# Ten dot products of the adaptive parameters of a two-block model, moved from the first block into the second

## The chip, the cores and the metric

The kernel runs on one core of a Trainium2 chip: TensorE (PE) for matmuls, VectorE (DVE), ScalarE (ACT) and GpSimd (POOL) for the rest, SyncE (SP) for most of the loads. The metric is the device time of one execution in microseconds.

## The reference, cut to what matters

Two transformer blocks follow each other on 256 tokens of width 2048. The second block scales and shifts its inputs by parameters that depend on a condition vector alone, not on the tokens: `silu(cond) @ w + b`, for the condition `c` of the latent tokens and `c_ctx` of the context tokens, for each of two layers.

```python
def ada_params(cond, w, b):                      # w: 2048 x 6144, for each of two layers
    mod = jax.nn.silu(cond) @ w + b
    return jnp.split(mod, 3, axis=-1)            # shift, scale, gate

x = first_block(x, ...)       # projections, rotary attention, a recurrence, output product,
                              # then expert rows chosen by a search and gathered from two tables
for layer in range(2):        # second block
    sh_l, sc_l, g_l = ada_params(c, ada_w[layer], ada_b[layer])
    sh_c, sc_c, g_c = ada_params(c_ctx, ada_w[layer], ada_b[layer])
    xm_l = x_lat * (1.0 + sc_l) + sh_l           # scale and shift: needed before the projections
    xm_c = x_ctx * (1.0 + sc_c) + sh_c           # context: layer 0 only
    ...                                          # l_q, l_k, l_g, l_v, l_u, l_o, l_zp, l_z, mixing
    x_lat = layer_norm(ALPHA * x_lat + g_l * (y_l @ w_out), ...)   # gate: needed only at the end
```

The parameters of one layer are 6144 numbers, 48 groups of 128: groups 0 to 15 are the shift, 16 to 31 the scale, 32 to 47 the gate. The context has no use for its gate.

## The kernel before

The adaptive weights lie in memory transposed, as tiles of 128 parameters by 2048. Tile (layer, k) holds group k of a layer, 1 MB. A tile's product with a condition vector is one instruction on DVE, `tensor_tensor_reduce` in `ada_dots` (L2074 to L2090), which the profile shows at L2088 as `CUSTOM_DVE_ANT_0` with a short `DVE_READ_ACCUMULATOR2_ANT` behind it. A tile whose third entry in `ADA_SEQ` is True is *dual*: it is multiplied by both condition vectors, in two instructions. Any other tile has one. There are 96 tiles, 32 of them dual, so 128 instructions whatever the order.

`ADA_SEQ` is the order of the tiles, `ADA_FIRST` says how many are worked off at each of twelve places of the first block's DVE code, and `ADA_AT` how many stand behind each of the four slots of a weight chunk in the second block. The tiles of the first block are loaded by POOL's queue (`ada_loads`, L730 to L743) into places that are free at the time, listed in `ADA_PLACE`; their number is `ADA_LAT`. From there on the tiles go through the ring: four slots of 1 MB that SP fills in one fixed order (L696 to L716) with all weights. Load n waits until what load n - 4 brought is used up; for a tile that is its dot.

The stages that matter here, in order:

- Rotary stages. DVE scales and rotates queries and keys, half of the tokens at a time (places `rope0` before, `rope1` between and `rope2` behind the halves), then copies the transposed parts head by head (L2279 to L2283). The attention's scores follow (L2298).
- Output product. Four chunks of 512 columns; PE L1021, then transposes L1098 of the new rows. DVE adds each chunk to X (`out_add`, L2332), with the dots of `w_out0` to `w_out3` between (L2339 and L2352). A matmul in full fp32 is two records in the trace.
- Query heads and search. PE L1130 and L1141; DVE takes the dots of `search` (L2366) and then chooses the top 16. The rows of two tables are gathered from there on, until about 1720 us.
- Second block. A weight is split for accuracy: ACT copies its high half (L1476), DVE subtracts to get the low half (`split_lo`, L2102; for l_u to l_z POOL does it), and PE takes three products (L903). A chunk is four slots of two pieces each. `split_lo` does for each slot: two low halves, a `conv_unit` of an earlier chunk where there is one (L2465 to L2467), then the dots of `ADA_AT`. `l_q`, `l_k` and `l_v` have two chunks each, `w_even` four. `l_g` is a small gate weight, with its dots at L2620. The weights of `l_k` and `l_v` are shared with the context's and carry the names `in_c_k` and `in_c_v` in the trace. After `w_even` the norm of `post` (L2821 to L2850) ends the layer, and the transposes L1380 begin the next.

The lines that say how the work is spread:

```python
107 ADA_SEQ = [(0, _k, True) for _k in range(16)] + [(0, _k, False) for _k in range(32, 40)]
108 ADA_SEQ += [(0, _k, True) for _k in range(16, 32)] + [(0, _k, False) for _k in range(40, 48)]
112 ADA_FIRST = {"in": 8, "in_x0": 4, "in_x1": 2, "conv": 2, "rope0": 1, "rope1": 3, "rope2": 4,
113              "w_out0": 4, "w_out1": 4, "w_out2": 4, "w_out3": 4, "search": 2}
```

## Time and profile before

| | us |
|---|---|
| median of 3 runs | 2619.73 (2617.78 to 2621.02) |
| profiled execution | 2618.13 |
| its span | 2616.3 |

| stage, from - to (us) | what runs |
|---|---|
| 0 - 150 | input projections, 16 dual tiles |
| 150 - 225 | rotary stages, eight single tiles |
| 225 - 271 | attention |
| 271 - 373 | output product, 16 dual tiles |
| 373 - 400 | first query head, search, two single tiles |
| 400 - 1720 | row gathers and their products |
| 1740 - 1860 | l_q, l_k, l_g, l_v 0 |
| 2142 - 2230 | w_even and its norm |
| 2230 - 2616 | odd layer and output |

A row of the timeline shows the start, the length, engine, line, operation and tiles, then the count, and in brackets the engine's idle time before it with what ended that. Neighbouring records on PE and DVE overlap by up to a tenth of a microsecond, so the spacing of the starts, not the length, is what one costs. A row of the chain is start, length and what it was.

### The profile page before, as it was taken

Reading aid. Unit: us, or ns where it says so; the run is one execution under the profiler, and the core shown is the slowest. Engines: PE = TensorE matmul, PEld = TensorE weight load, DVE = VectorE, ACT = ScalarE, POOL = GpSimd, SP = SyncE. Lnnn points to the kernel's source line nnn. Section 1 sums busy time; section 2 is a strip of 40 time slices with the busy share of each in tenths; the row PEclk is TensorE's granted clock in tenths of the full one; section 3 lists DMA queues with packets and bytes.
Section 4 is the critical chain, followed back from the end, with each engine's and each line's share of the span. In section 5 each row is a group of like instructions: output and inputs, shape, how many; then the busy total and the mean of one; then the engine's idle time right before and its main releaser. Section 6 shows DMA issues by size and latency. Waiting matters only on the chain.

```text
span 2616.3 us, 23133 instructions
## 1 busy us (share of the span) xinstructions
PE 2164.5 (83%) x8406; PEld 1472.8 (56%) x8406; DVE 2060.7 (79%) x2582; ACT 679.9 (26%) x1149; POOL 1131.0 (43%) x641
## 2 busy tenths in 40 slices
PE   8999999896004666778787888799999999999997
PEld 5877558655001222344443333379778887788886
DVE  6886797988997997687886777789865689777666
ACT  2054110100000000332540000133524444544343
POOL 0000003555586678767887776730255640000000
PEclk9999999898557888888779989899999999999999
DMA  9663879999999999999999999978843458777552
GB/s 377 263 263 129 331 290 375 387 421 422 407 422 421 397 408 420 420 417 407 359 310 404 393 387 370 386 290 310 321 188 129 172 204 349 292 293 289 192 202 104
DMA packets 126977, 845.16 MB, mean 323 GB/s; under 512 B 22507, under 2 KB 23019, under 8 KB 25195
## 3 DMA queue, kind: packets, MB, share of 16 engines
q0 software_dynamic: 79776, 513.13, 49.1%
q1 hardware_dynamic: 43344, 308.04, 30.9%
q10 hardware_dynamic: 3744, 22.52, 2.2%
q8 instruction: 67, 1.10, 0.2%
q14 instruction: 46, 0.38, 0.0%
HBM read 909.36 MB, written 2.10 MB: 348 GB/s over the span
## 4 chain that ended last, share of the span: by engine, by line
PE 46%; DMA 18%; DVE 16%; POOL 12%; issue 7%; ACT 1%; DVEq 0%; POOLq 0%; ACTq 0%; SPq 0%
PE psum L903 23%; DMA W<-in_peer_v,HT 7%; PE psum L1021 4%; DMA W<-in_peer_u,W 4%; POOL W L785 4%; POOL W L783 4%; DVE W L2450 3%; PE psum L859 3%; PE psum L1186 3%; PE psum L835 3%; POOL early_rows L783 3%; DMA early_rows<-in_peer_v,HT 3%; DVE early_rows L2450 2%; DMA early_rows<-in_peer_u,W 2%; DVE X L2592 2%
## 5 line engine op out<-in xcount | busy, mean ns | idle before, releaser
L1186 PE MATMUL psum<-W,HT 128*128 128x512 f32 x536 | 299.2, 711 | 311.0 <-ACT HT L1683 175.5
L903 PE MATMUL psum<-split,hi 128*128 128x512 f32 x1664 | 514.7, 390 | 3.1 <-DVE split L2102 3.1
L2450 DVE CUSTOM_DVE_ANT_0 W<-W,XN 128x2048 f32<-128x2048 f32 x148 | 335.1, 2290 | 73.3 <-DMA W<-in_peer_u,W 70.9
L1476 ACT ACTIVATE split<-ring 128x1024 fp32r<-128x1024 f32 x272 | 282.6, 1057 | 409.1 <-PE psum L903 290.3
L1186 PEld LDWEIGHTS psum<-W,HT 128*128 128x128 f32 x536 | 117.5, 228 | 479.9 <-issue 471.8
L785 POOL DMA_INDIRECT W<-in_peer_v,HT x173 | 317.3, 1834 | 91.4 <-issue 49.0
L903 PEld LDWEIGHTS psum<-split,hi 128*128 128x128 f32 x1664 | 311.6, 188 | 68.7 <-issue 3.2
L2102 DVE TENSOR_TENSOR split<-ring,split 128x1024 fp32r<-128x1024 f32 x206 | 247.0, 1224 | 124.1 <-ACT split L1476 123.1
L783 POOL DMA_INDIRECT W<-in_peer_u,W x148 | 249.2, 1684 | 179.4 <-DVE W L2450 71.1
L2592 DVE SCALAR_TENSOR_TENSOR X<-W,X 128x2048 f32<-128x2048 f32 x106 | 251.7, 2375 | 67.6 <-DMA W<-in_peer_v,HT 64.8
L2450 DVE CUSTOM_DVE_ANT_0 early_rows<-early_rows,XN 128x2048 f32<-128x2048 f32 x108 | 244.6, 2290 | 50.4 <-DMA early_rows<-in_peer_u,W 49.3
L759 POOL TENSOR_TENSOR split<-ring,split 128x1024 fp32r<-128x1024 f32 x66 | 168.7, 2582 | 220.8 <-ACT split L1476 220.6
L783 POOL DMA_INDIRECT early_rows<-in_peer_u,W x108 | 188.0, 1740 | 120.5 <-DVE W L2450 80.5
L1186 PE MATMUL psum<-early_rows,HT 128*128 128x512 f32 x320 | 179.3, 714 | 68.5 <-DMA early_rows<-in_peer_v,HT 66.9
L1683 ACT ACTIVATE HT<-cst,W 128x128 f32<-128x128 f32 x107 | 41.4, 396 | 556.1 <-PE psum L1186 550.8
L785 POOL DMA_INDIRECT early_rows<-in_peer_v,HT x83 | 162.3, 1955 | 43.8 <-issue 24.7
L1186 PEld LDWEIGHTS psum<-early_rows,HT 128*128 128x128 f32 x320 | 70.6, 230 | 166.4 <-issue 162.7
L903 PE MATMUL psum<-split,lo_odd 128*128 128x512 f32 x384 | 149.5, 389 | 0.0
L859 PE MATMUL psum<-HT,ring 128*128 128x256 f32 x640 | 138.8, 379 | 0.0
L859 PEld LDWEIGHTS psum<-HT,ring 128*128 128x128 f32 x640 | 121.5, 190 | 16.5
L2592 DVE SCALAR_TENSOR_TENSOR X<-early_rows,W,X 128x2048 f32<-128x2048 f32 x43 | 101.1, 2351 | 34.7 <-DMA early_rows<-in_peer_v,HT 33.9
L795 POOL TENSOR_TENSOR lo<-W,hi 128x512 fp32r<-128x512 f32 x4 | 5.9, 1487 | 276.5 <-ACT hi L1458 276.5
(409 smaller groups left out, 3582.6 us busy)
## 6 DMA issues: line engine op xcount, KB each, us to landing
ring<-in_ada SPq DMA_DIRECT2D x54, 1024.0 KB, 5.9
ring<-in_odd SPq DMA_DIRECT2D x48, 1024.0 KB, 6.0
ring<-in_peer_v SPq DMA_DIRECT2D x24, 1024.0 KB, 9.4
XN<-in_ada POOLq DMA_DIRECT2D x19, 1024.0 KB, 7.0
ring<-in_w_out SPq DMA_DIRECT2D x16, 1024.0 KB, 6.4
ring<-in_pq SPq DMA_DIRECT2D x16, 1024.0 KB, 9.6
ring<-in_c_v SPq DMA_DIRECT2D x16, 1024.0 KB, 9.5
ring<-in_c_k SPq DMA_DIRECT2D x16, 1024.0 KB, 7.3
```

The costliest lines, as they stand in the source:

```text
L759: nc.gpsimd.tensor_tensor(split[:, to + 1024:to + 2048], ring[:, at:at + 1024], split[:, to:to + 1024], ALU.subtract).then_inc(sem("lo_poo ...
L783: nc.gpsimd.indirect_dma_start(row, None, t["peer_u"], at).then_inc(full, 16)
L785: nc.gpsimd.indirect_dma_start(row, None, t["peer_v"], at, bounds_check=NKEY * NKEY - 1, oob_is_err=False).then_inc(full, 16)
L835: m = nc.tensor.matmul(o[tt][:, 0:width], lhs[:, k, tt * P:(tt + 1) * P], sl[:, kk * width:(kk + 1) * width], start=(k == 0), stop=(k == s ...
L859: m = nc.tensor.matmul(o[a][:, S * b:S * b + S], sl[:, kk * 512 + m4 * P:kk * 512 + m4 * P + P], rhs[:, k, :], start=(k == 0 and b == 0), ...
L903: m = nc.tensor.matmul(dst, lhs, rhs, start=(k == 0 and b == 0 and not (features and i % 2)), stop=(k == KD - 1 and b == 2 and not (featur ...
L1021: m = nc.tensor.matmul(out_units[name, 2 * c + tt], MIX[:, k, tt * P:(tt + 1) * P], sl[:, kk * 512:kk * 512 + 512], start=(k % 8 == 0), st ...
L1186: m = nc.tensor.matmul(o[0][c], DIAG[n % DIAGS], row[:, 512 * c:512 * c + 512], start=(n == 0), stop=False)
L1476: A(split[:, 2048 * (n % PIECES):2048 * (n % PIECES) + 1024], ring[:, at:at + 1024], ACT.Copy)\
L2102: TT_(split[:, to + 1024:to + 2048], ring[:, at:at + 1024], split[:, to:to + 1024], ALU.subtract)\
L2450: V.tensor_tensor_reduce(out=row, in0=row, in1=xn3[:, tt, :], scale=1.0, scalar=0.0, op0=ALU.mult, op1=ALU.add, accum_out=PACT[:, c:c + 1])\
L2592: STT(x3[:, tt, :], row, PACT[:, c:c + 1], x3[:, tt, :], ALU.mult, ALU.add)\
```

## The change

The sequence is sorted so that all 32 dual tiles come first. The first block works off 32 tiles, all dual, where it had 42, of which 32 were dual; ten single gate tiles (k = 32 to 39, then 40 and 41) that stood there now go through the ring. In instructions: the rotary stages have 12 where they had 8, the output product 20 where it had 32, the search none where it had 2; the first block has 64 in all where it had 74. In the second block `l_q` 0 gets one more, `l_q` 1 and `l_k` 0 two more each, `l_k` 1 one, `l_g` two, and the third and fourth chunk of `w_even` one each. What is computed stays the same.

```diff
-ADA_SEQ = [(0, _k, True) for _k in range(16)] + [(0, _k, False) for _k in range(32, 40)]
-ADA_SEQ += [(0, _k, True) for _k in range(16, 32)] + [(0, _k, False) for _k in range(40, 48)]
+ADA_SEQ = [(0, _k, True) for _k in range(32)] + [(0, _k, False) for _k in range(32, 48)]
...
-ADA_FIRST = {"in": 8, "in_x0": 4, "in_x1": 2, "conv": 2, "rope0": 1, "rope1": 3, "rope2": 4,
-             "w_out0": 4, "w_out1": 4, "w_out2": 4, "w_out3": 4, "search": 2}
+ADA_FIRST = {"in": 8, "in_x0": 4, "in_x1": 2, "conv": 2, "rope0": 1, "rope1": 2, "rope2": 3,
+             "w_out0": 3, "w_out1": 3, "w_out2": 2, "w_out3": 2, "search": 0}
...
-ADA_PLACE += [("early", "xn0", "xn1")[_n % 3] for _n in range(8)]
-ADA_PLACE += [("early", "xc", "xn0", "xn1")[_n % 4] for _n in range(18)]
+ADA_PLACE += [("early", "xn0", "xn1")[_n % 3] for _n in range(6)]
+ADA_HALF = len(ADA_PLACE)
+ADA_PLACE += [("early", "xc", "xn0", "xn1")[_n % 4] for _n in range(10)]
...
-ADA_AT["l_q", 0] = (0, 0, 0, 2)
+ADA_AT["l_q", 0] = (0, 0, 0, 3)
 for _step in (("l_q", 1), ("l_k", 0), ("l_k", 1)):
-    ADA_AT[_step] = (1, 1, 1, 0)
+    ADA_AT[_step] = (1, 1, 1, 1)
 ADA_AT["l_v", 0] = ADA_AT["l_v", 1] = (1, 1, 1, 1)
-ADA_AT["l_g", 0] = (3,)
+ADA_AT["l_g", 0] = (5,)
+ADA_AT["l_q", 1] = ADA_AT["l_k", 0] = (1, 1, 1, 2)
...
-    ADA_AT["w_even", _c] = ((0, 0, 1, 1), (1, 1, 1, 1), (1, 1, 1, 0), (1, 1, 1, 0))[_c]
+    ADA_AT["w_even", _c] = ((0, 0, 1, 1), (1, 1, 1, 1), (1, 1, 1, 1), (1, 1, 1, 1))[_c]
```

The remaining lines of the diff put `ADA_HALF` and the new counts in place of the numbers 24, 25 and 68 in the conditions of POOL's loads and of the choice of the condition vector's copy. The new file is one line longer ahead of `build`, so its lines are one higher.

On DVE, behind the second rotary half (`rope2`), before. The names on the left of the arrow are what is written; `XN` and `early_rows` hold tiles:

```order
L2258 TENSOR_SCALAR W<-W 128x2048
L2088 ISA XN,ada<-XN,early_rows,col 128x2048
L2088 ISA ada 128x1
L2088 ISA XN,ada<-XN,early_rows,col 128x2048
L2088 ISA ada 128x1
L2088 ISA early_rows,ada<-early_rows,col 128x2048
L2088 ISA ada 128x1
L2088 ISA XN,ada<-XN,early_rows,col 128x2048
L2088 ISA ada 128x1
L2261 TENSOR_TENSOR W<-W 128x2048
```

and now:

```order
L2089 ISA early_rows,ada<-early_rows,col 128x2048
L2089 ISA ada 128x1
L2089 ISA early_rows,ada<-early_rows,col 128x2048
L2089 ISA ada 128x1
L2089 ISA early_rows,ada<-XN,early_rows,col 128x2048
L2089 ISA ada 128x1
L2089 ISA XN,ada<-XN,early_rows,col 128x2048
L2089 ISA ada 128x1
L2089 ISA early_rows,ada<-XN,early_rows,col 128x2048
L2089 ISA ada 128x1
L2089 ISA XN,ada<-XN,early_rows,col 128x2048
L2089 ISA ada 128x1
```

Four dots of four tiles became six dots of three dual tiles, between the same two neighbours.

On DVE, at the last slot of `l_k` 0, behind which `l_k` 1 begins, before (`split` is a low half, `W<-psum` the convolution of the queries):

```order
L2102 TENSOR_TENSOR split<-ring,split 128x1024 x2
L2465 TENSOR_SCALAR W<-psum,col 128x256
L2466 SCALAR_TENSOR_TENSOR W<-psum,col,W 128x255
L2467 SCALAR_TENSOR_TENSOR W<-psum,col,W 128x255
L2102 TENSOR_TENSOR split<-ring,split 128x1024 x2
```

and now:

```order
L2103 TENSOR_TENSOR split<-ring,split 128x1024 x2
L2466 TENSOR_SCALAR W<-psum,col 128x256
L2467 SCALAR_TENSOR_TENSOR W<-psum,col,W 128x255
L2468 SCALAR_TENSOR_TENSOR W<-psum,col,W 128x255
L2089 ISA ring,ada<-ring,XN,col 128x2048
L2089 ISA ada 128x1
L2089 ISA ring,ada<-ring,XN,col 128x2048
L2089 ISA ada 128x1
L2103 TENSOR_TENSOR split<-ring,split 128x1024 x2
```

Two dots stand between the last query convolution and the first low half of the next chunk.

On SP, from the end of `l_k` 1 over `l_g` to the first chunk of `l_v`, before:

```order
L716 DMA ring<-in_c_k 128x2048
L716 DMA ring<-in_ada 128x2048
L716 DMA ring<-in_c_k 128x2048
L716 DMA ring<-in_c_g 128x256
L716 DMA ring<-in_ada 128x2048 x3
L716 DMA ring<-in_c_v 128x2048
```

and now:

```order
L717 DMA ring<-in_c_k 128x2048
L717 DMA ring<-in_ada 128x2048
L717 DMA ring<-in_c_k 128x2048
L717 DMA ring<-in_ada 128x2048
L717 DMA ring<-in_c_g 128x256
L717 DMA ring<-in_ada 128x2048 x5
L717 DMA ring<-in_c_v 128x2048
```

One tile more before the gate weight and two more behind it, so the first value weight is four loads behind the second of five tiles, where it was four behind the gate weight.

## Rows read from the trace of the kernel before

**Rows 1.** The page's first part: busy time of each engine over the span.
```profile
PE 2164.5 (83%) x8406; PEld 1472.8 (56%) x8406; DVE 2060.7 (79%) x2582; ACT 679.9 (26%) x1149; POOL 1131.0 (43%) x641
```

**Rows 2.** Timeline of DVE, rotary stages to the first score: start us, us.
```profile
157.32 0.17 DVE L2234 COPY stat<-stat 128x8 f32<-128x8 f32 x1 [7.82 <-ACT X L1521]
...
205.22 2.35 DVE L2088 CUSTOM_DVE_ANT_0 XN<-XN,early_rows,col 128x2048 f32<-128x2048 f32 x1 [2.61 <-DMA XN<-in_ada]
...
207.50 2.28 DVE L2261 TENSOR_TENSOR W<-W 128x2048 f32<-128x2048 f32 x1
...
210.99 0.42 DVE L2283 COPY XN<-psum 64x256 f32<-64x256 f32 x1
...
226.30 0.35 DVE L2298 SCALAR_TENSOR_TENSOR W<-psum,stat,cst 128x128 f32<-128x128 f32 x1
```

**Rows 3.** Timeline of PE, output product and first query head.
```profile
309.78 27.63 PE L1021 MATMUL psum<-ring,W 128*128 128x512 f32 x64
337.25 1.04 PE L1098 MATMUL psum<-cst,X 128*128 128x128 f32 x8
...
373.33 5.34 PE L1130 MATMUL psum<-HT,ring 128*128 128x256 f32 x24
```

**Rows 4.** Groups of PE, 271.5 to 373; then 315 to 340: PE, PEld, DVE, ACT, POOL.
```profile
L1021 PE MATMUL psum<-ring,W 128*128 128x512 f32 x224 | 97.0, 592 | 0.0
...
315.00:340.00 25.00, 25.00 (x66) 11.56 (x65) 24.27 (x25) 2.39 (x6) 2.64 (x5) 1.00 0.86 321
```

**Rows 5.** Timeline of DVE, output product and search.
```profile
328.42 2.35 DVE L2088 CUSTOM_DVE_ANT_0 early_rows<-early_rows,col 128x2048 f32<-128x2048 f32 x1 [0.26 <-DVE X L2332]
...
351.23 2.35 DVE L2088 CUSTOM_DVE_ANT_0 early_rows<-early_rows,col 128x2048 f32<-128x2048 f32 x1 [0.26 <-DVE X L2332]
...
372.68 1.65 DVE L2332 SCALAR_TENSOR_TENSOR X<-psum,stat,X 128x512 f32<-128x512 f32 x2 [0.68 <-PE psum L1021]
...
391.42 0.49 DVE L2380 MAX8 W<-W 128x8 f32<-128x128 f32 x2 [1.25 <-ACT W L1634]
```

**Rows 6.** Timeline of PE, transposes of the fourth head, first product matmuls.
```profile
212.88 0.60 PE L1007 MATMUL psum<-cst,W 128*64 128x128 f32 x4
...
227.44 3.70 PE L1021 MATMUL psum<-ring,W 128*128 128x512 f32 x8
```

**Rows 7.** The chain that ended last, second block: start us, us, what.
```profile
1739.68 57.87 PE psum L903 x480
...
1822.49 6.89 DMA ring<-in_c_v
...
1839.03 8.30 DMA ring<-in_c_v
...
2177.98 42.25 PE psum L903 x180
```

**Rows 8.** Timeline of DVE, l_q to l_v, the rows with its longer waits.
```profile
1753.65 0.48 DVE L2465 TENSOR_SCALAR W<-psum,col 128x256 f32<-128x256 f32 x1 [0.89 <-PE psum L903]
...
1776.69 0.48 DVE L2465 TENSOR_SCALAR W<-psum,col 128x256 f32<-128x256 f32 x1 [0.56 <-PE psum L903]
...
1799.64 2.36 DVE L2102 TENSOR_TENSOR split<-ring,split 128x1024 fp32r<-128x1024 f32 x2 [2.98 <-ACT split L1476]
...
1830.49 2.36 DVE L2102 TENSOR_TENSOR split<-ring,split 128x1024 fp32r<-128x1024 f32 x2 [1.21 <-ACT split L1476]
```

**Rows 9.** Timeline of ACT: the silu of the queries.
```profile
1796.75 1.92 ACT L1834 ACTIVATE W<-W 128x2048 f32<-128x2048 f32 x1 [6.76 <-DVEq L2471]
```

**Rows 10.** Waits of DVE, 1744 to 1880: us in total, times, longest.
```profile
DVE split L2102 <- ACT split L1476: 9.9, 5, 3.7
```

**Rows 11.** Timeline of DVE, last chunk of w_even and the norm.
```profile
2197.86 2.36 DVE L2102 TENSOR_TENSOR split<-ring,split 128x1024 fp32r<-128x1024 f32 x2
...
2223.36 0.68 DVE L2827 CUSTOM_DVE_ANT_0 W<-psum,W 128x512 f32<-128x512 f32 x1
...
2227.52 0.16 DVE L2844 TENSOR_TENSOR stat<-stat 128x2 f32<-128x2 f32 x1 [0.56 <-ACT XN L1790]
```

More of the change, by code:

```diff
@@ L738, in ada_loads @@
                         wait_unit(pool, ("xT", 7))
-                    if name in ("xn0", "xn1") and n >= 24:
+                    if name in ("xn0", "xn1") and n >= ADA_HALF:
                         wait_unit(pool, ("score", 2 * NH - 1))
@@ L745, in _ @@
             pool.wait_ge(sem("x_loaded1"), 16)
-            ada_loads(0, 25)
+            ada_loads(0, ADA_HALF + 1)
             pool.wait_ge(sem("rec_out"), 2)
-            ada_loads(25, ADA_LAT)
+            ada_loads(ADA_HALF + 1, ADA_LAT)
             def split_lo(name, c, first=0, last=8):
@@ L2083, in ada_dots @@
                         dve.wait_ge(sem("cond_ready"), 3)
-                    rows = COND1 if n < ADA_LAT else [COND_LAT[(n >= 68) + (n >= 80)]]
+                    rows = COND1 if n < ADA_LAT else [COND_LAT[(n >= 66) + (n >= 80)]]
                     if dual and n:
```

## The prediction

> **What bounds the kernel now.** I read the chain that ended last first, then, stage by stage, the timelines of TensorE (PE) and VectorE (DVE) for the wait that ends last. Over the whole span DVE is at 79% and PE at 83% [rows 1], which decides nothing, because the change touches five stages, each with its own limit. A *dot* here is one full-width L2088 instruction on DVE, 128x2048. Its record is 2.35 us long, but the next work starts 2.27 us after it (205.22 to 207.50, [rows 2]), so 2.27 us is its price. A *dual* tile costs two.
>
> In the **output product** PE never stops. One chunk is 64 matmul records in 27.5 us (309.78 to 337.25) plus 0.9 us of transposes, so 28.3 us, and over the whole stage its 224 records have an idle time of 0.0 [rows 3, 4]. DVE is nearly as full (24.27 of 25 us, [rows 4]), but its chunk is only 22.8 us (328.42 to 351.23, [rows 5]), of which eight dots are 18.2. It runs ahead of PE, and at the end of the stage it waits for PE (0.68 us at 372.68). So PE bounds this stage, and the first query head behind it. After the two dots of the search DVE again stands still, 1.25 us at 391.42, until ACT has copied the first scores, which come from PE [rows 5]. Then come the row gathers, full of DMA to about 1700 us; nothing in them is changed, so they move as a block.
>
> In the **rotary stages** DVE feeds the attention. From 207.50 it works without a gap through the eight heads to the first score at 226.30, and PE is at its heels [rows 2, 6].
>
> In the **second block** up to the gates, DVE and PE run almost in step. PE takes 480 matmuls in 57.87 us, 0.1206 us each [rows 7]: a chunk of 192 is 23.1 us. A slot costs DVE 2.28 us for two low halves and 1.55 us for a convolution (1776.69 is the first of its three instructions, [rows 8]), so a chunk with three dots is 4 x 3.83 + 3 x 2.27 = 22.1 us. From the second chunk of l_k on, PE waits for DVE, and the chain goes through DVE.
>
> **The change, part by part.** *Removed, output product and search:* 12 dots fewer in the product (32 to 20) and 2 in the search, 14 x 2.27 = 31.8 us of DVE. The cover is PE: 28.3 us a chunk against DVE's 22.8, and behind the last addition (372.68) the head's matmuls fill PE from 373.33 on [rows 3, 5]. I take 0, because no PE row of the stage has a gap; the bounds are 0 and, should all of it come off the path, -31.8. The tiles' loads leave POOL's queue, which has nothing else to do before the gathers.
>
> A rule of the Trainium skill speaks against this reading. The row of this stretch shows weight loads (LDWEIGHTS) busy for 11.56 of 25 us beside matmuls at 25 [rows 4]. "Perfetto Trace Analysis", section "Identifying the Most-Contended Engine", calls matmul busy time a bad measure and LDWEIGHTS busy the better one; by it PE has headroom here and DVE, at 97%, would be the engine to relieve, which would give the time of the first rival in place of 0. No row shows a PE gap that it would need.
>
> *Added, rotary:* eight single dots in three steps become twelve (six dual tiles): one more before the first half, one more between the halves, two more behind the second. The first falls into 7.82 us in which DVE waits for ACT (157.32): 0. The second delays what follows by 2.27. Behind the second half six dots take the place of four and of a wait of 2.61 us for a tile (205.22) [rows 2]; that wait goes, since POOL can issue the three tiles used there as soon as the dots of three tiles earlier are done, the last of them before 180 us. On DVE: 2.27 + 2 x 2.27 - 2.61 = +4.2 us at 207.50. PE's second transposes of the fourth head, at 212.88 [rows 6], reuse the bank that DVE frees by its second copy of head one, at 210.99 + 0.42 = 211.41: 1.5 us of slack, so PE moves by 2.7. The next tie is the product's first matmuls at 227.44, which need the gains that DVE has ended when it takes the first score at 226.30: 1.1 us of slack, so 3.1. I take **+2.9**, between the two; bounds 0 and 4.2.
>
> *Added, second block up to the gates:* 1, 2, 2, 1 and 2 dots in l_q 0, l_q 1, l_k 0, l_k 1 and l_g: 8 x 2.27 = 18.2 us in a queue that is full. They can hide in DVE's own waits [rows 8]: 0.89 (for PE, 1753.65), 0.56 (for PE, 1776.69) and 2.98 (for ACT, 1799.64). The last is the silu of the queries, 1.92 us [rows 9], and one high half, both behind the last query convolution; two of the new dots stand right behind that convolution, so they cover it. Together 4.4. The 1.21 us at 1830.49 stays: the value weights' load starts when a slot four loads earlier is released and lands 6.9 us later [rows 7]; that release is now the second dot of five, and moves with them. 18.2 - 4.4 = **+13.8**. Behind it PE's l_v 1, ACT and DVE's scans follow one from the other, so it passes on whole. SP's queue has eight more loads of 1 MB, each for a slot that a dot frees; two low halves, a convolution and a pair of dots are 8.4 us, against 6.9 us of landing and 1 us for the high half. Bounds: 18.2 less all of DVE's waits in this stretch, 9.9 for ACT's high halves [rows 10] and 1.4 for PE (0.89 and 0.56), is 6.9; 18.2 with none hidden and 4 us of waits for the ring is 22.
>
> *Added, w_even:* one dot at the end of each of the last two chunks. PE has run 180 matmuls in 42.25 us from 2177.98, 2.82 us a piece of twelve, and wants the last chunk at 2177.98 + 8 x 2.82 = 2200.5; DVE has its first low half at 2197.86 + 1.14 = 2199.0 [rows 7, 11]. So the first dot alone costs PE 0.8 us. But both stand before DVE's last additions, which it reaches at 2223.36 just as PE ends the unit: +4.55. ACT's squares give back about 0.5 of it (DVE waits 0.56 for them at 2227.52). I take **+4.0**; bounds 0.8 and 4.6.
>
> *Unchanged:* the tiles of l_v, l_u and the odd stage, and all before the rotary step.
>
> Sum: 0 + 2.9 + 13.8 + 4.0 = +20.7 us. The profiled execution took 2618.13 us (span 2616.3 and 1.8 around it), so 2638.8; the median of the three runs is 1.6 us higher, by which it would be 2640.4. I forecast **2639**.
>
> **The rivals.** *The relief pays* (faster). If the product's matmuls really wait for DVE's additions and the banks these free, and the records don't show it, the 14 dots come off: 2618.1 + 20.7 - 31.8 = 2607. It decides from the point where DVE's chunk is longer than PE's. DVE's 97% speaks for it (and the rule above), 22.8 us against 28.3 against it. 5%.
>
> *The extra dots hide* (slower, by less). DVE's waits between 1744 and 1880 take up all they can: 6.9, with 2.9 and with 0.8 in w_even: 10.6, so 2629. Against it: the longest wait, 3.7 us [rows 10], lies before l_v 1, behind a chunk that gets nothing new. 10%.
>
> *Almost nothing* (within 0.2%). All low bounds at once, 0 + 0 + 6.9 + 0.8, are 2626, and some more must hide in later waits. 4%.
>
> *The ring starves* (slower still). With two tiles behind one slot a weight load waits for a dot and lands late. One landing here took 8.3 us [rows 7]; at that the pair of dots no longer covers it, and at l_q 1, l_k 0, l_g and both new places I'd add 1.5 us each, an estimate from 8.3 + 1 - 8.4 with DMA busier: 2638.8 + 7.5 = 2646. 10%.
>
> **How the numbers follow.** The forecast, 2631 to 2645, has 71%. With hiding and ring the range is 2627 to 2647. A measurement of this kernel can tell about 0.2%, 5.2 us, from no change, so "same" is 2614.5 to 2625: 4%. Faster 5%, slower 91%.
>
> **What would show it.** Right: the product's 224 records still take 97 us with 0.0 idle, and DVE shows waits for PE in it; the first score on DVE comes some 4 us later, the product and the first gather about 3 us later; from l_q 0 to the start of l_v 1 it is some 14 us more, with PE waiting for DVE in l_q 1 and l_k 0; the transposes behind w_even 4 us more. Wrong: a first gather earlier than before; PE's chunks in l_q 1 and l_k 0 still at 23.1 us; DVE waiting for DMA at each pair of dots.

## The result, and the profile after

| | before | after |
|---|---|---|
| median, four runs each, of one comparison | 2618.76 (2614.93 to 2621.02) | 2636.12 (2635.33 to 2638.57) |
| ratio, 95% interval | | 1.0069 (1.0052 to 1.0087) |
| span of the profiled execution | 2616.3 | 2634.8 |

The changed kernel is slower, by 17.4 us in the medians and 18.5 us between the two profiled spans. The forecast was 2639 with a range of 2627 to 2647, so it held. In a second comparison, below, the changed kernel had a median of 2638.49 against 2617.12.

The page's first line, against [rows 1]:

```profile
PE 2159.1 (82%) x8406; PEld 1473.5 (56%) x8406; DVE 2061.6 (78%) x2582; ACT 681.6 (26%) x1149; POOL 1121.1 (43%) x631
```

DVE has the same 2582 instructions: dots were moved, none added. No engine is busy more than 1.7 us longer than before, so nearly all of the 18.5 us is waiting. POOL has ten instructions fewer, the loads of the ten tiles, which SP now does.

**Rotary stages.** DVE's timeline of the changed kernel, against [rows 2] (start, length, what; in brackets the wait before it):

```profile
156.09 0.17 DVE L2235 COPY stat<-stat 128x8 f32<-128x8 f32 x1 [5.55 <-ACT X L1522]
...
196.83 2.35 DVE L2089 CUSTOM_DVE_ANT_0 early_rows<-early_rows,col 128x2048 f32<-128x2048 f32 x1
...
208.19 2.35 DVE L2089 CUSTOM_DVE_ANT_0 XN<-XN,early_rows,col 128x2048 f32<-128x2048 f32 x1
...
210.46 2.29 DVE L2262 TENSOR_TENSOR W<-W 128x2048 f32<-128x2048 f32 x1
...
229.56 0.35 DVE L2299 SCALAR_TENSOR_TENSOR W<-psum,stat,cst 128x128 f32<-128x128 f32 x1
```

The wait for ACT has shrunk from 7.82 to 5.55 us: the extra dot there is hidden. The six dots behind the second half, from 196.83 to 208.19, stand without a gap; the 2.61 us of waiting for a tile is gone. This execution reached the stage 1.23 us earlier than that of before (156.09 against 157.32), so L2262 at 210.46 against 207.50 is 2.96 + 1.23 = 4.2 us later in its stage, as forecast. PE's timeline there, against [rows 6]:

```profile
214.43 0.63 PE L1008 MATMUL psum<-cst,W 128*64 128x128 f32 x4 [2.61 <-DVE XN L2284]
214.90 3.28 PE L992 MATMUL psum<-HT,ring 128*128 128x256 f32 x8
...
230.70 3.70 PE L1022 MATMUL psum<-ring,W 128*128 128x512 f32 x8
```

PE waits exactly where the forecast put it, at the fourth head's second transposes, for DVE's copy of head one (L2284). Corrected for the early start, 214.43 is 2.8 us late. But the eight matmuls behind the wait take 3.28 us, where the same eight take 1.89 before each of the other heads from 203 us on. The view of stretches shows why (from, to, length, then busy time of PE, PEld, DVE, ACT and POOL, the granted clock, the DMA share and GB/s):

```profile
213.00:216.00 3.00, 1.57 (x8) 1.36 (x9) 2.72 (x6) 0.00 (x0) 0.00 (x0) 0.87 0.00 0
216.00:219.00 3.00, 3.00 (x13) 2.42 (x12) 2.61 (x6) 0.05 (x1) 0.00 (x0) 0.56 0.02 5
```

The clock had been at 1.00, 2.4 GHz, over the whole stretch from 150 us; behind 2.6 us of waiting it was 0.87 and then 0.56, so for a part of these stretches it was at its lower level, 1.2 GHz. That cost 1.4 us in the eight matmuls (3.28 for 1.89) and 0.3 us in the transposes behind them (the next head's matmuls start 4.28 us after 214.90, and 2.60 us after the same point before): 1.7 us in all, and 2.8 + 1.7 is the 4.5 us by which the stage is longer.

**Output product and head.** Groups and timeline of PE in the changed kernel, against [rows 3, 4], then DVE's timeline, against [rows 5]:

```profile
L1022 PE MATMUL psum<-ring,W 128*128 128x512 f32 x224 | 97.0, 592 | 0.0
...
376.60 5.34 PE L1131 MATMUL psum<-HT,ring 128*128 128x256 f32 x24
```

```profile
283.33 2.35 DVE L2089 CUSTOM_DVE_ANT_0 early_rows<-early_rows,col 128x2048 f32<-128x2048 f32 x1 [8.95 <-DMA X<-in_x]
...
341.66 1.00 DVE L2042 TENSOR_SCALAR HT<-psum,col 128x256 f32<-128x256 f32 x2 [6.64 <-PE psum L1099]
...
394.69 0.49 DVE L2381 MAX8 W<-W 128x8 f32<-128x128 f32 x2 [5.80 <-ACT W L1635]
```

The product takes its 97.0 us again, with an idle time of 0.0. DVE starts the stage late in both kernels, behind a wait for DMA (8.95 us here, 8.91 before). What it was spared it now waits: 6.64 us in one chunk for PE, 5.80 in the search where it was 1.25. From the first product matmuls to the first gather on POOL it is 172.7 us in both kernels, 230.70 to 403.42 here and 227.44 to this row before:

```profile
400.14 1.00 POOL L783 DMA_INDIRECT W<-in_peer_u,W  x1 [38.91 <-DVEq L2432]
```

The relief is worth nothing, to a tenth of a microsecond.

**Second block.** The chain that ended last, against [rows 7]; DVE's timeline, against [rows 8]; what PE waited for, 1744 to 1895 (in total, times, longest):

```profile
1838.03 7.53 DMA ring<-in_c_v
...
1855.21 6.95 DMA ring<-in_c_v
...
1875.18 22.04 PE psum L904 x96
```

```profile
1835.64 2.35 DVE L2089 CUSTOM_DVE_ANT_0 ring<-ring,XN,col 128x2048 f32<-128x2048 f32 x1
...
1838.13 2.35 DVE L2089 CUSTOM_DVE_ANT_0 ring<-ring,XN,col 128x2048 f32<-128x2048 f32 x1
...
1846.67 2.36 DVE L2103 TENSOR_TENSOR split<-ring,split 128x1024 fp32r<-128x1024 f32 x2 [1.21 <-ACT split L1477]
...
1873.81 2.36 DVE L2103 TENSOR_TENSOR split<-ring,split 128x1024 fp32r<-128x1024 f32 x2 [2.35 <-ACT split L1477]
```

```profile
PE psum L904 <- DVE split L2103: 9.7, 6, 3.2
```

DVE's waits of 0.89, 0.56 and 2.98 us are gone, the 1.21 us before l_v 0 stands as it did, and PE waits 9.7 us for DVE where it had waited 3.1. The stretch is measured from the row at 1739.68 in [rows 7]. That is not PE's first matmul of l_q 0: three of its eight pieces, 72 matmuls, run before it from 1729.45 on, with waits for DVE between them. From 1739.68 on PE ran without a gap up to l_k 1, so its fourth piece is the mark for the start in every kernel. It is at 1741.22 in the changed kernel, and l_v 1 begins at 1875.18: 133.96 us, against 120.66 before (1739.68 to 1860.34):

```profile
1860.34 22.03 PE psum L903 x96
```

The clock fell in this stretch too. The rows from 1777 to 1800 in the changed kernel, and then in e2_second, which has the same second block (columns as above):

```profile
1777.00:1800.00 23.00, 20.39 (x147) 20.21 (x147) 22.53 (x26) 8.27 (x8) 0.00 (x0) 0.85 0.91 358
```

```profile
1777.00:1800.00 23.00, 20.07 (x163) 19.49 (x162) 22.30 (x26) 7.36 (x8) 0.00 (x0) 1.00 0.97 360
```

Here it cost nothing: the whole stretch is 134.0 us in the changed kernel and 133.9 in e2_second, where the clock stayed at 1.00 up to the wait before l_v 0. PE waits for DVE here, so a slower PE waits less.

**w_even.** DVE's timeline, against [rows 11], then the chain:

```profile
2206.69 2.36 DVE L2103 TENSOR_TENSOR split<-ring,split 128x1024 fp32r<-128x1024 f32 x2 [1.82 <-ACT split L1477]
...
2215.58 2.36 DVE L2103 TENSOR_TENSOR split<-ring,split 128x1024 fp32r<-128x1024 f32 x2
...
2242.65 0.68 DVE L2828 CUSTOM_DVE_ANT_0 W<-psum,W 128x512 f32<-128x512 f32 x1
```

```profile
2248.97 5.65 PE psum L1381 x32
```

The same row before:

```profile
2230.13 6.02 PE psum L1380 x32
```

The transposes come 18.8 us later, of which 14.8 had gathered by the start of l_v 1, so 4.0 arose here. Up to the end it stays at that (18.5).

### The profile page after: what moved, and what is told of

The parts are those of the page before. It is cut to its first block, busy times and chain, and to the rows that moved or that the text cites. A ratio compares the mean times of both kernels' runs of the same rounds, so it can differ in the third digit from the quotient of the medians.

```text
span 2634.8 us, 23131 instructions
## 1 busy us (share of the span) xinstructions
PE 2159.1 (82%) x8406; PEld 1473.5 (56%) x8406; DVE 2061.6 (78%) x2582; ACT 681.6 (26%) x1149; POOL 1121.1 (43%) x631
## 4 chain that ended last, share of the span: by engine, by line
PE 40%; DVE 22%; DMA 20%; POOL 10%; issue 6%; ACT 1%; DVEq 0%; POOLq 0%; ACTq 0%; SPq 0%
PE psum L904 19%; DMA W<-in_peer_v,HT 9%; DMA W<-in_peer_u,W 5%; PE psum L1022 4%; POOL W L784 4%; PE psum L1187 3%; PE psum L836 3%; DVE W L2451 3%; POOL W L786 3%; DVE X L2593 3%; DMA early_rows<-in_peer_v,HT 3%; POOL early_rows L784 3%; DVE split L2103 2%; DVE ring L2089 2%; DMA early_rows<-in_peer_u,W 2%
## 5 line engine op out<-in xcount | busy, mean ns | idle before, releaser
L1187 PE MATMUL psum<-W,HT 128*128 128x512 f32 x536 | 289.7, 692 | 322.6 <-ACT HT L1684 177.1
L786 POOL DMA_INDIRECT W<-in_peer_v,HT x173 | 305.9, 1768 | 92.3 <-issue 47.2
L760 POOL TENSOR_TENSOR split<-ring,split 128x1024 fp32r<-128x1024 f32 x66 | 168.7, 2582 | 234.1 <-ACT split L1477 233.9
L784 POOL DMA_INDIRECT early_rows<-in_peer_u,W x108 | 193.7, 1793 | 116.8 <-DVE W L2451 74.7
L786 POOL DMA_INDIRECT early_rows<-in_peer_v,HT x83 | 162.1, 1953 | 43.1 <-issue 23.8
L904 PE MATMUL psum<-split,lo_even 128*128 128x512 f32 x320 | 125.5, 392 | 0.0
L2089 DVE CUSTOM_DVE_ANT_0 ring<-ring,XN,col 128x2048 f32<-128x2048 f32 x48 | 113.4, 2368 | 14.2 <-DMA ring<-in_ada 11.0
```

What stands on the lines that cost most here:

```text
L760: nc.gpsimd.tensor_tensor(split[:, to + 1024:to + 2048], ring[:, at:at + 1024], split[:, to:to + 1024], ALU.subtract).then_inc(sem("lo_poo ...
L784: nc.gpsimd.indirect_dma_start(row, None, t["peer_u"], at).then_inc(full, 16)
L786: nc.gpsimd.indirect_dma_start(row, None, t["peer_v"], at, bounds_check=NKEY * NKEY - 1, oob_is_err=False).then_inc(full, 16)
L904: m = nc.tensor.matmul(dst, lhs, rhs, start=(k == 0 and b == 0 and not (features and i % 2)), stop=(k == KD - 1 and b == 2 and not (featur ...
L1187: m = nc.tensor.matmul(o[0][c], DIAG[n % DIAGS], row[:, 512 * c:512 * c + 512], start=(n == 0), stop=False)
L2089: V.tensor_tensor_reduce(out=COND_JUNK if i else w_, in0=w_, in1=rows[i], scale=1.0, scalar=column("ada_b", 48 * l + k), op0=ALU.mult, op1 ...
```

## The experiments

There are eleven runs in three sets, each beside runs of the kernel before on the same chip. e5_changed is the changed kernel again and e6_rope222 is e4_rope222 again, so nine kernels are new. Since the gathers differ by some microseconds from run to run, the lengths of the stages in each profile tell more than the medians. In the table *rotary* is from the first PE record of the stage (L859, 163.20 us in the trace before) to the first product matmuls; *product* from there to the first gather; *gathers* from there to the fourth piece of l_q 0 on PE (1739.68 before); *l* to l_v 1 on PE; *w_even* from DVE's first dot in it to the transposes. The stretch between *l* and *w_even*, in which no kernel changes a thing, was 284.2 to 285.6 us, and 281.9 in e3_noprod. All in microseconds; lines in the changed files are shifted by a few.

| kernel | rotary | product | gathers | l | w_even | ratio (95%) |
|---|---|---|---|---|---|---|
| before | 64.2 | 172.7 | 1339.5 | 120.7 | 85.3 | |
| changed | 68.7 | 172.7 | 1337.8 | 134.0 | 89.3 | 1.0069 (1.0052 to 1.0087) |
| e5_changed | 68.8 | 172.7 | 1341.8 | 134.3 | 89.6 | 1.0078 (1.0056 to 1.0100) |
| e1_first | 67.3 | 172.7 | 1340.1 | 119.6 | 86.1 | 1.0017 (1.0008 to 1.0026) |
| e2_second | 64.2 | 172.7 | 1343.4 | 133.9 | 89.4 | 1.0074 (1.0062 to 1.0086) |
| e3_noprod | 64.2 | 173.3 | 1340.2 | 119.6 | 85.7 | 1.0004 (0.9996 to 1.0013) |
| e4_rope222 | 64.2 | 172.7 | 1339.1 | 133.7 | 88.9 | 1.0070 (1.0057 to 1.0083) |
| e6_rope222 | 64.3 | 172.7 | 1339.4 | 133.5 | 88.8 | 1.0059 (1.0038 to 1.0081) |
| e7_four_more | 64.3 | 178.6 | 1340.1 | 119.6 | 85.4 | 1.0028 (1.0016 to 1.0041) |
| e8_three_back | 64.2 | 172.7 | 1341.4 | 118.8 | 85.7 | 0.9991 (0.9979 to 1.0003) |
| e9_weven | 64.2 | 172.7 | 1341.0 | 119.6 | 88.3 | 1.0008 (0.9999 to 1.0018) |
| e10_lg | 64.3 | 172.7 | 1339.5 | 124.3 | 86.3 | 1.0025 (1.0015 to 1.0034) |
| e11_six | 64.3 | 172.7 | 1338.5 | 130.1 | 86.6 | 1.0032 (1.0018 to 1.0047) |

**The first block alone.** The first block's tables as changed, the second's as before, and the ten tiles in neither:

```diff
-ADA_SEQ = [(0, _k, True) for _k in range(32)] + [(0, _k, False) for _k in range(32, 48)]
+ADA_SEQ = [(0, _k, True) for _k in range(32)] + [(0, _k, False) for _k in range(42, 48)]
...
+            seq(V.memset(ada_v[:, 0, 32:42, 0], 1.0))
             ada_dots(ADA_FIRST["in"])
```

> The first block as in the changed kernel (64 dots, rotary stages 12, product 20, search none), the second block as before; the ten gate tiles of layer 0 (groups 32 to 41) are left out altogether, their results set to a constant, so their ten dots and 10 MB of loads stand nowhere. Cover theory (PE covers all dots of the product): only the rotary stages count, +2.8 us of waiting at the fourth head and 1.7 us of matmuls at a lower granted clock behind it, as the profile of the changed kernel has them: +4.5 us against before, and the product's records take 97.0 us with no idle time. Rival, the relief pays: 14 dots of 2.27 us come off, -31.8 + 4.5 = -27 us. Rival, the gathers swallow a late start (in the changed kernel the shift was 3.3 us at the first gather and 1.6 behind the last): 0 to +2 us.

Measured: 2621.50 against 2616.58, +4.9 in the medians, +4.4 by the ratio (2.1 to 6.8). The relief would have shown as -27; it is refuted. PE around the fourth head:

```profile
215.37 0.63 PE L1011 MATMUL psum<-cst,W 128*64 128x128 f32 x4 [2.63 <-DVE XN L2288]
215.84 1.89 PE L995 MATMUL psum<-HT,ring 128*128 128x256 f32 x8
...
230.20 3.70 PE L1025 MATMUL psum<-ring,W 128*128 128x512 f32 x8 [0.17 <-DVE W L2280]
```

The same wait, but here the eight matmuls take 1.89 us: the clock did not fall (1.00 in this stretch). The rotary stages are 3.1 us longer without the lower clock and 4.5 with it. So of the expected 4.5 the 1.7 for the clock did not come, and the time alone, +4.4, would not have shown it. The 0.17 us is the second tie that the forecast had named (the gains before the product's first matmuls, 3.1 us); it shows only when the clock has not made PE later still.

**The second block alone.** The first block exactly as before, the second as changed, filled up with ten tiles that are multiplied a second time:

```diff
-ADA_SEQ += [(0, _k, True) for _k in range(16, 32)] + [(0, _k, False) for _k in range(40, 48)]
+ADA_SEQ += [(0, _k, True) for _k in range(16, 32)] + [(0, _k, False) for _k in (40, 41)]
+ADA_SEQ += [(0, _k, False) for _k in range(32, 48)]
```

> The first block as before with all its 74 dots; the second block as in the changed kernel, with eight more dots in l_q to l_g and two more in w_even. The ten tiles for them are gate tiles multiplied a second time, so nothing is relieved in the first block. Cover theory: l_q to the start of l_v 1 +13.3 us and w_even +4.0 us, as between the two profiles: +17.3 us. Relief rival: if taking x us of dots from the first block had paid x, this kernel would be x slower than the changed one, which is 17 to 18 us above before; with x = 31.8 it would be at +50 us. If the moved first block costs 4.5 us, this kernel is that much faster than the changed one.

Measured: 2636.81 against 2616.58, ratio 1.0074, so +19.4 (16.2 to 22.5). The +50 us of the relief rival is out. With the whole first block still in place the kernel is as slow as the changed one. So most of the loss is made in the second block, and nothing was earned to set against it. The two stages in the table are 133.9 and 89.4 us, as in the changed kernel. By the stages this kernel should be 3 to 4.5 us faster than the changed one; its time does not show that (the gathers of its profile, 1343.4 us, are the longest of all), and the interval is too wide to deny it.

**No dots in the product at all.** The kernel before without the 18 tiles of product and search (34 dots; their results are a constant):

```diff
-ADA_SEQ += [(0, _k, True) for _k in range(16, 32)] + [(0, _k, False) for _k in range(40, 48)]
+ADA_SEQ += [(0, _k, False) for _k in range(42, 48)]
...
-             "w_out0": 4, "w_out1": 4, "w_out2": 4, "w_out3": 4, "search": 2}
+             "w_out0": 0, "w_out1": 0, "w_out2": 0, "w_out3": 0, "search": 0}
```

> The kernel before with all dots of the product and the search left out: 18 tiles, 34 dots, 77 us of DVE and 18 MB of loads gone (their results set to a constant). Rotary stages and second block as before. Cover theory: PE sets the product's time, so 0 us, at most 1 to 2 us faster from the search, where DVE waits for ACT behind its two dots; product 97.0 us with no idle time on PE. Relief rival: what DVE is spared comes off, at the least the 31.8 us of the change's 14 dots, at most 77 us. Rival, the loads matter (18 MB less on the queues): the weights of the product are there earlier, but PE did not wait for them, so 0 as well.

Measured: 2617.50 against 2616.58, ratio 1.0004 (0.9996 to 1.0013). PE's group in this kernel:

```profile
L1023 PE MATMUL psum<-ring,W 128*128 128x512 f32 x224 | 97.0, 592 | 0.0
```

77 us of DVE and 18 MB of loads taken away from a stage in which DVE was 97% busy, and the stage is not shorter. "Perfetto Trace Analysis" of the Trainium skill, section "Identifying the Most-Contended Engine", which the forecast had weighed, would have had PE with headroom here. The trace and this run disagree with it for these full-precision matmuls.

**Rotary dots spread otherwise.**

On the changed kernel:

```diff
-ADA_FIRST = {"in": 8, "in_x0": 4, "in_x1": 2, "conv": 2, "rope0": 1, "rope1": 2, "rope2": 3,
+ADA_FIRST = {"in": 8, "in_x0": 4, "in_x1": 2, "conv": 2, "rope0": 2, "rope1": 2, "rope2": 2,
```

> The changed kernel with its six dual tiles of the rotary stages as 2, 2 and 2 instead of 1, 2 and 3: two more dots before the first half, where DVE waited 5.55 us for ACT, two fewer behind the second. Theory on the rotary stages: DVE reaches the heads 4.5 us earlier, PE's wait of 2.6 us at the fourth head and the low clock behind it go, the first score comes 3 to 4.5 us earlier; 4.5 us faster than the changed kernel, about +14 us against before. Rival, the gathers swallow it: no faster than the changed kernel (+17 to +18) though the first gather starts earlier. Rival, the tile for the second pair is not there yet at the first place: DVE waits for DMA there and the gain shrinks.

Measured: 2635.38 against 2616.58, ratio 1.0070, so +18.3 (14.9 to 21.7) where some +14 was expected. The stage is back at 64.2 us and PE has no wait in it, as the theory has it, but the time is that of the rival, by which the gathers swallow the gain. The changed kernel had been timed in another comparison, though. So both were run side by side:

> The changed kernel once more, beside the others on the same chip. The parts measured alone say 4.4 (first block, 95% interval 2.1 to 6.8) and 19.4 (second block, 16.2 to 22.5), together +23.8 us; the changed kernel had +17 to +18 us (13.6 to 22.8) in its own comparison. If the parts add up, +20 to +23 us here; if the gathers swallow a late start, +17 to +18.

> The changed kernel with its rotary tiles as 2, 2, 2, again, now beside the changed one. Its first profile showed the first gather at 399.8 us where the changed kernel has 403.4, and no wait of PE at the fourth head. If a late first gather costs its lateness, 3 us faster than the changed kernel (up to 4.5 where that one also meets the low clock behind its wait); if the gathers swallow it, the same.

Measured: 2638.49 and 2634.29 against 2617.12, ratios 1.0078 and 1.0059. The changed kernel is 4.2 us slower than its rearranged version in the medians, 4.5 us in the rotary column. The intervals overlap, but stage and median agree. The gathers don't swallow a late start: they took 1337.8 and 1341.8 us in two executions of the same changed kernel, 1337.8 to 1343.4 over all thirteen profiles, whether they began at 399 or at 405. What looked in the first pair of profiles like a gain of 1.7 us in them was that scatter. With the parts at 4.4 and 19.4 us the sum is 23.8; the changed kernel had +18 and, here, +20.4 (14.7 to 26.2). The intervals allow that the parts add up, and the stages do: 3.1 to 4.5 in the rotary stages, 14.3 in l (133.9 in the mean of the five profiles with the changed second block, against 119.6) and 3.3 in w_even make 20.7 to 22.1.

**More dots in the product.** If DVE has 5.5 us to spare in each chunk, one more dot in each should be free:

```diff
-             "w_out0": 4, "w_out1": 4, "w_out2": 4, "w_out3": 4, "search": 2}
+             "w_out0": 5, "w_out1": 5, "w_out2": 5, "w_out3": 5, "search": 2}
```

This is on the kernel before, with four gate tiles multiplied a second time there.

> The kernel before with one dot more in each of the four chunks of the product (36 instead of 32 there; four gate tiles are multiplied a second time), all else as before. DVE's chunk becomes 22.8 + 2.3 = 25.1 us against PE's 28.3. Theory A, the chunk decides: 0 us, PE's 224 records still take 97.0 us without a gap. Theory B, the end decides: DVE starts this stage late (it waits 8.9 us before its first dot), catches up with PE just at the last addition (0.68 us of waiting), so 9.1 us more put that addition 8.4 us later; the query head behind it needs its rows, PE waits 3 to 5 us there and the search, which is DVE's, starts up to 8 us later: +4 to +8 us.

Measured: 2624.39 against 2617.12, ratio 1.0028, +7.3 (4.2 to 10.7). DVE at the last addition, then PE at the first head:

```profile
380.14 1.65 DVE L2338 SCALAR_TENSOR_TENSOR X<-psum,stat,X 128x512 f32<-128x512 f32 x2
```

```profile
372.38 3.62 PE L1136 MATMUL psum<-HT,ring 128*128 128x256 f32 x16
380.20 3.40 PE L1136 MATMUL psum<-HT,ring 128*128 128x256 f32 x8 [4.21 <-DVEq L2054]
383.44 1.04 PE L1104 MATMUL psum<-cst,X 128*128 128x128 f32 x8
```

The product's own records are still 97.0 us without a gap. But DVE starts the stage late and catches up 5.5 us a chunk: before, it drew level just at the last addition (0.68 us of waiting in [rows 5]). With 9.1 us more it comes to that addition 8.4 us later (380.14 against 372.68, in an execution that was 0.95 us ahead), PE waits 4.21 us for its rows (4.4 from start to start), and then loses 1.5 us to the lower clock (3.40 us for eight matmuls in place of 1.89). The product column is 5.9 us longer, which is the sum. So the stage has a margin in one direction only: dots taken away bring nothing, dots added cost at once.

**The opposite of the change.** Three dots of the second block moved into DVE's wait for ACT ahead of the rotary half:

```diff
-ADA_SEQ = [(0, _k, True) for _k in range(16)] + [(0, _k, False) for _k in range(32, 40)]
+ADA_SEQ = [(0, _k, True) for _k in range(18)] + [(0, _k, False) for _k in range(32, 39)]
...
-ADA_FIRST = {"in": 8, "in_x0": 4, "in_x1": 2, "conv": 2, "rope0": 1, "rope1": 3, "rope2": 4,
-             "w_out0": 4, "w_out1": 4, "w_out2": 4, "w_out3": 4, "search": 2}
+ADA_FIRST = {"in": 8, "in_x0": 4, "in_x1": 2, "conv": 2, "rope0": 2, "rope1": 3, "rope2": 4,
+             "w_out0": 4, "w_out1": 5, "w_out2": 5, "w_out3": 4, "search": 2}
...
+ADA_AT["l_k", 1] = (1, 0, 1, 0)
+ADA_AT["l_v", 0] = (1, 0, 1, 1)
...
-ADA_AT["l_g", 0] = (3,)
+ADA_AT["l_g", 0] = (2,)
```

> The opposite of the change, on the kernel before: three gate dots move from l_k 1, l_g and l_v 0 (one each) into the first block, where the wait of DVE for ACT ahead of the first rotary half (7.8 us) takes them: two dual tiles stand there instead of one single one, the product keeps its 32 dots (two dual tiles fewer, four single ones more) and the search its two. Balance theory: nothing in the first block moves, since three dots are 6.8 us of the 7.8; from l_q 0 to the start of l_v 1 it is 2 to 3 us less, not 6.8, because PE has only 3.1 us of waiting for DVE in that stretch; -2 to -3 us against before. Rival, each dot in the second block costs its 2.3 us: -6.8 us. Rival, the singles in the product's place make DVE late: 0 or slower.

Measured: 2615.92 against 2617.12, ratio 0.9991 (0.9979 to 1.0003): no difference that can be told. It is the only version whose median lies below the kernel before, and it doesn't beat it. DVE's wait at the place, then the chain before l_v 1:

```profile
157.48 0.17 DVE L2243 COPY stat<-stat 128x8 f32<-128x8 f32 x1 [0.99 <-ACT X L1530]
```

```profile
1826.57 10.91 PE psum L938 x96
1837.48 10.92 PE psum L912 x48
1848.43 1.06 ACT split L1485
...
1860.47 19.55 PE psum L912 x85
```

The three dots hide as meant: the rotary and product columns don't move. The l column is 118.8, only 0.8 us below the 119.6 of four of the five profiles with an unchanged second block up to l_v. My 2 to 3 us were too much. Relieved of DVE, the chain stays on PE from 1803 to 1848.40; from there to l_v 1 it is ACT's for most of 12 us. The rival of -6.8 us is outside the interval.

**The second block's parts.** On the kernel before, with repeated tiles, first the two dots of `w_even`, then the two of `l_g`, then the other six:

```diff
-    ADA_AT["w_even", _c] = ((0, 0, 1, 1), (1, 1, 1, 1), (1, 1, 1, 0), (1, 1, 1, 0))[_c]
+    ADA_AT["w_even", _c] = ((0, 0, 1, 1), (1, 1, 1, 1), (1, 1, 1, 1), (1, 1, 1, 1))[_c]
```

> The kernel before with one dot more at the end of the third and of the fourth chunk of w_even, nothing else changed; the two are tiles of layer 1 multiplied a second time. From the profiles: w_even to the transposes of the next layer 4.0 us longer, as in the changed kernel; the rest of the run unchanged: +4.0 us. Bounds: 0.8 if the second dot hides behind PE's end, 4.6 if nothing is given back. Rival, the wait of PE for the first low halves of the last chunk: +0.8 only.

Measured: 2620.56 against 2617.19, ratio 1.0008 (0.9999 to 1.0018). The time alone can't tell this from nothing; the stage can. The last chunk's first low half and the last addition:

```profile
2199.04 2.36 DVE L2106 TENSOR_TENSOR split<-ring,split 128x1024 fp32r<-128x1024 f32 x2
...
2226.58 0.68 DVE L2831 CUSTOM_DVE_ANT_0 W<-psum,W 128x512 f32<-128x512 f32 x1
```

That is 27.5 us where [rows 11] has 25.5 (2197.86 to 2223.36), and the third chunk is 2.2 us longer too (23.42 for 21.25): the two dots cost 2.0 and 2.2 us. The column is 88.3, only 2.4 us above the mean of 85.9 of the seven profiles without them: the second chunk, which gets no dot, happened to be 1.2 us shorter than in their mean, and some of the cost comes back behind the last addition. The rival of +0.8 us is out by the stage.

```diff
-ADA_AT["l_g", 0] = (3,)
+ADA_AT["l_g", 0] = (5,)
```

> The kernel before with five dots in l_g instead of three, nothing else changed; the two are gate tiles multiplied a second time. DVE is full there and the first value weight's load starts with the second of five dots: 2 x 2.27 = 4.5 us more to the first low half of l_v 0, plus up to 0.9 us of small waits between the five dots, since four tiles in a row arrive only every 2.5 us (in the changed kernel 0.1 to 0.2 us before each). Then up to 1.3 us may be given back ahead of l_v 1, where DVE's wait for ACT was 3.7 us before and 2.4 us in the changed kernel. So the start of l_v 1 is 4 to 5.5 us later, +4 to +5.5 us in all. Rival, hidden by the load's latency: 0 to 1 us.

Measured: 2623.51 against 2617.19, ratio 1.0025, +6.5 (3.9 to 8.9); l is 124.3, so 4.7 us more than 119.6, within the 4 to 5.5. The rival of 0 to 1 us is out. DVE's longer waits there:

```profile
1828.99 2.35 DVE L2092 CUSTOM_DVE_ANT_0 ring<-ring,XN,col 128x2048 f32<-128x2048 f32 x1 [0.44 <-DMA ring<-in_ada]
...
1835.01 2.36 DVE L2106 TENSOR_TENSOR split<-ring,split 128x1024 fp32r<-128x1024 f32 x2 [1.22 <-ACT split L1480]
```

```diff
-ADA_AT["l_q", 0] = (0, 0, 0, 2)
+ADA_AT["l_q", 0] = (0, 0, 0, 3)
 for _step in (("l_q", 1), ("l_k", 0), ("l_k", 1)):
-    ADA_AT[_step] = (1, 1, 1, 0)
+    ADA_AT[_step] = (1, 1, 1, 1)
+ADA_AT["l_q", 1] = ADA_AT["l_k", 0] = (1, 1, 1, 2)
```

> The kernel before with six more dots in l_q 0 (1), l_q 1 (2), l_k 0 (2) and l_k 1 (1), l_g left at three; the six are gate tiles multiplied a second time. 6 x 2.27 = 13.6 us, of which 4.4 hide in DVE's own waits (0.89, 0.56 and 2.98 us): the first low half of l_v 0 comes 9.2 us later, l_v 1 8 to 9.2 us, +8 to +9.2 us in all. Rival, nothing hides: +13.6. Rival, PE's wait is what counts and the dots of l_q 1 and l_k 0 hide up to PE's 23.1 us a chunk: +6.

Measured: 2626.59 against 2617.19, ratio 1.0032, +8.4 (4.7 to 12.3); l is 130.1, 10.5 above 119.6, more than the 8 to 9.2. DVE's waits in l_k 1 and l_v 0:

```profile
1811.39 2.36 DVE L2107 TENSOR_TENSOR split<-ring,split 128x1024 fp32r<-128x1024 f32 x2 [0.49 <-ACT split L1481]
...
1838.47 2.36 DVE L2107 TENSOR_TENSOR split<-ring,split 128x1024 fp32r<-128x1024 f32 x2 [1.21 <-ACT split L1481]
```

Of the 2.98 us only 2.49 hid (0.49 is left), so 13.6 - 0.89 - 0.56 - 2.49 = 9.7 us at l_v 0, where the traces have 10.0 (against e9_weven); the rest came in the last wait before l_v 1 (2.97 us against 2.47 in e9_weven). The two rivals, +13.6 and +6, are out by the stage; of the time's interval only the first is outside. 4.7 + 10.5 = 15.2, near the 14.3 of all eight together. A tile's dot and its load came together in all these runs. That DVE's work and not the load is what costs rests on its rows, which stand without gaps but for the waits shown; no run adds the loads alone.

## Why the prediction was right, point by point

**Product and search: 0, measured 0.0.** The argument from PE's row without a gap held in the changed kernel, in e1_first and, with all 34 dots gone, in e3_noprod. The cover was read as 5.5 us a chunk, which is right for a chunk and not for the stage: e7_four_more showed that DVE, late from the start, uses all four of them to catch up: it does not run "ahead of PE", as the forecast has it, but draws level at the last addition. The forecast did not need this, since it only took away.

**Rotary: +2.9, measured 3.1 and 4.5.** DVE's +4.2 and the place and size of PE's slip (2.7, measured 2.8) came as worked out, and so did the second tie at 3.1. What was missing is a term: after its wait PE ran part of the next head at the lower clock, 1.7 us in both profiles of the changed kernel and 0 in e1_first. The term was sized for full clock only, and 4.5 lies above its upper bound of 4.2.

**l_q 0 to l_g: +13.8, measured 13.3 between the two profiles and 14.3 against the other executions.** The stretch before was 120.7 us in the profile that the forecast used and 119.6 in e1_first, e3_noprod, e7_four_more and e9_weven; it had one landing of 8.30 us in its chain [rows 7], and the changed kernel had 6.95 at that place. The forecast's 13.8 lies between the two because two small errors cancel, which is luck. At the first low half of l_v 0 the shift is 14.6 rather than 13.8: DVE's dots in l_g stand 2.49 us apart (1835.64, 1838.13) instead of 2.27, since five tiles follow one another and each arrives that much after the last. That is a trace of the ring rival; it costs 0.8 us, not 7.5 (five places at 1.5 us, though the rival's own figures, 8.3 + 1 - 8.4, give 0.9). Ahead of l_v 1 1.3 us were then given back by the shorter landing. That 1.21 us would stay before l_v 0 was right to the hundredth.

**w_even: +4.0, measured 4.0 between the profiles, 3.3 in the mean.** The five profiles with the change's two dots have 88.8 to 89.6 in this column, the seven without them 85.3 to 86.6 (mean 85.9). e9_weven, with nothing else changed, has 2.4. Each dot delays DVE by about 2.2 us. Behind the last addition, in the wait for the squares, 0.45 us comes back against the profile of before, as assumed, but 0.9 against five of the six others without the dots: this wait is 0.95 or 0.96 us there, 0.56 in [rows 11], and gone in all kernels with the dots. The remaining difference lies in the waits for landings (1.82 us at 2206.69 in the changed kernel, 0.81 at the same place in e9_weven), which vary from run to run. The term was sized a little high.

**The sum: +20.7, measured +17.4 in the medians (+18 by the ratio) and +21.4 (+20.4) in the second comparison.** The profiled execution after took 2636.6 us with the 1.8 around its span, 2.2 below the forecast of 2638.8: its rotary stages began 1.2 us earlier and its gathers were 1.7 us shorter, both scatter, l_q 0 to l_v 1 was 0.5 less and the odd layer 0.3, while the rotary stages took 1.6 more than I had allowed, by the lower clock. The stages themselves, against the other executions, give 20.7 to 22.1. So the mechanism was right, stage by stage, and that the first comparison came within 3 us of 2639 although the clock's 1.7 us was missing from the sum is in part luck.

**The rivals.** The relief pays: refuted by e1_first, e2_second and e3_noprod. The extra dots hide (+10.6): no, PE waits 9.7 us for DVE. Almost nothing: no. The ring starves: a tenth of it is there.

## What to carry to other kernels

Ask of each place that gets or loses work which engine the next one waits for, and give each place its own price: taking the same 2.27 us instruction out of the product paid 0; put ahead of the first rotary half it cost 0, in the second block about 1.8, and one more in each product chunk cost 1.5 apiece. In this kernel an engine that was 97% busy beside one that never stopped was worth no relief. And a margin read from one turn of a loop is not the margin of the loop: look at who is late when it begins, and at the wait behind its last turn.

## What the runs showed of the hardware that I had not expected

- PE's granted clock can fall after a single wait of under 3 us, and the wait's length alone does not decide whether it does. The thirteen profiles have 28 waits of PE of more than 2 us in the rotary stages, the first query head and the second block up to l_v 1. Before each the clock was 1.00. Behind 18 of them it was 0.50 to 0.72 over the next 3 us, the shortest being 2.21 us (e4_rope222); behind the other ten it stayed at 1.00, the longest being 3.12 us (e5_changed). The same wait in the rotary stages, 2.61 and 2.64 us, was followed by a fall in both profiles of the changed kernel, and one of 2.63 us in e1_first was not. Why is open.
- The price depends on who sets the pace. In the rotary stages a fall cost 1.7 us, in the query head of e7_four_more (behind 4.21 us) 1.5. In the second block, where PE waits for DVE, it cost nothing that can be seen: l is 133.7 and 133.5 us in e4_rope222 and e6_rope222, with three falls each before l_v 1, and 133.9 and 134.3 in e2_second and e5_changed, with one and none.
- The lower level is half of the full one: behind the wait in the changed kernel the next head's first transposes start 0.43 us apart, where they start 0.22 apart at a clock of 1.00. "TensorE: Matmul & The Clock Gate" of the Trainium skill gives in Part 1 1.2 GHz for an idle and 2.4 GHz for a busy array. The 18 falls agree, each with PE idle just before; the ten waits without a fall show that such a wait need not be enough.
- The product column of e3_noprod is 0.6 us longer than the others: POOL had stood still for 202 us before its first gather, where it had been 39 us before and 83 us in the changed kernel, and the gather started 0.94 us after the end of DVE's last index instruction, where it was 0.33 in both others. That the long pause is the reason is not shown, since only this run has it. POOL's timeline in e3_noprod:

```profile
401.07 1.00 POOL L785 DMA_INDIRECT W<-in_peer_u,W  x1 [201.84 <-DVEq L2435]
```
